# The expert loop of a two-block transformer: 23 items of 128 tokens become 31 items of 64, with each expert's weights loaded once

## The reference, cut to what matters

```python
g_idx = jnp.argmax(t @ w_group + b_group, axis=-1)
top_v, top_i = lax.top_k(e_in_group, 2)
for e in range(16):
    a = silu(t @ w_gate[e]) * (t @ w_up[e])      # 1024 -> 512, twice
    y = y + gates[:, e:e + 1] * (a @ w_down[e])  # 512 -> 1024
```

## Time and profile before

| what | value |
|---|---|
| median of 3 executions | 2894.31 us (2893.11 to 2896.62) |
| span of the profiled execution | 2900.2 us |
| TensorE busy in it | 2738.8 us, 94% |
| VectorE, ScalarE, GpSimd busy | 1274.2, 618.9, 486.6 us |
| moved by DMA | 403.19 MB, 139 GB/s over the span |

### The profile page before, as it was taken

How to read it: one execution, slowest core, us unless ns; L and a number is a source line. 1 busy time by engine, 2 the same in 40 slices (tenths; PEclk the granted TensorE clock), 3 DMA queues, 4 the chain that set the end, 5 groups by cost and what they waited for, 6 DMA issues and landing times.

```text
span 2900.2 us, 36551 instructions
## 1 busy us (share of the span) xinstructions
PE 2738.8 (94%) x14709; PEld 2101.4 (72%) x14709; DVE 1274.2 (44%) x2365; ACT 618.9 (21%) x1184; POOL 486.6 (17%) x515
## 2 busy tenths in 40 slices
PE   7999988897997899999999999999999999999998
PEld 4686755676853688788878877488887585788883
DVE  2072761656354111111132487276663342666651
ACT  2102012242412111111131255211110121211100
POOL 2062600554521000000010006101110001011010
PEclk8999988999998899999999999999999999999999
DMA  9311143243344999899972200122221321322220
GB/s 369 102 44 32 41 146 116 75 152 138 102 175 156 360 333 331 319 328 334 330 266 79 67 7 1 58 73 87 88 80 66 98 88 36 118 87 88 80 80 29
DMA packets 214917, 403.19 MB, mean 139 GB/s; under 512 B 13650, under 2 KB 123778, under 8 KB 205570
## 3 DMA queue, kind: packets, MB, share of 16 engines
q1 hardware_dynamic: 207586, 375.15, 37.7%
q10 hardware_dynamic: 4896, 17.83, 1.5%
q0 software_dynamic: 2304, 8.39, 0.7%
HBM read 369.88 MB, written 31.46 MB: 138 GB/s over the span
## 4 chain that ended last, share of the span: by engine, by line
PE 71%; issue 20%; DVE 3%; ACT 2%; DMA 2%; POOL 1%; SPq 0%; ACTq 0%; POOLq 0%; DVEq 0%
PE ps L2989 18%; PE ps L724 8%; PE ps L1770 6%; PE ps L3063 5%; PE ps L3046 4%; PE ps L2519 4%; PE ps L716 3%; PE ps L3327 3%; PE ps L2676 2%; PE ps L1198 2%; PE ps L415 2%; PE ps L1212 2%; PE ps L796 2%; DMA ring<-in_w_mod 1%; PE ps L2700 1%
## 5 line engine op out<-in xcount | busy, mean ns | idle before, releaser
L2076 PEld LDWEIGHTS ps<-arena,ring 128*128 128x128 f32 x2944 | 334.0, 193 | 14.0 <-issue 10.5
L2076 PE MATMUL ps<-arena,ring 128*128 128x128 f32 x2944 | 334.3, 276 | 3.0 <-DMA ring<-in_w_gate 3.0
L2989 PE MATMUL ps<-arena 128*128 128x256 f32 x1056 | 240.9, 386 | 8.3 <-DVE arena L3145 8.3
L2989 PEld LDWEIGHTS ps<-arena 128*128 128x128 f32 x1056 | 204.5, 194 | 37.5 <-issue 8.7
L724 PE MATMUL ps<-hT,ring 128*128 128x512 f32 x384 | 171.6, 601 | 3.8 <-ACT bet L1075 1.8
L1770 PE MATMUL ps<-ring,hT 128*128 128x512 f32 x384 | 169.7, 598 | 4.6 <-ACT hT L1805 2.4
L2094 PE MATMUL ps<-ring,arena 128*128 128x512 f32 x368 | 164.0, 598 | 1.8
L2989 PE MATMUL ps<-hT,ring 128*128 128x256 f32 x704 | 159.1, 379 | 0.0
L3063 PE MATMUL ps<-ring,arena 128*128 128x512 f32 x352 | 151.7, 592 | 0.0
L2365 DVE TENSOR_TENSOR arena<-arena,ps 128x512 f32<-128x512 f32 x23 | 15.8, 687 | 304.1 <-PE ps L2076 304.1
L2989 PEld LDWEIGHTS ps<-hT,ring 128*128 128x128 f32 x704 | 133.6, 190 | 18.1
(11 more groups left out here) (539 smaller groups left out, 4668.3 us busy)
## 6 DMA issues: line engine op xcount, KB each, us to landing
ring<-in_ada_w SPq DMA_DIRECT2D x48, 1024.0 KB, 5.0
ring<-in_w_gate SPq DMA_DIRECT2D x46, 1024.0 KB, 6.5
ring<-in_w_up SPq DMA_DIRECT2D x46, 1024.0 KB, 5.8
ring<-in_w_down SPq DMA_DIRECT2D x46, 1024.0 KB, 5.4
ring<-in_ffn_w_up SPq DMA_DIRECT2D x44, 1024.0 KB, 5.1
ring<-in_w_mod SPq DMA_DIRECT2D x24, 1024.0 KB, 7.9
ring<-in_w_in SPq DMA_DIRECT2D x18, 1024.0 KB, 8.9
ring<-in_attn_w_in SPq DMA_DIRECT2D x14, 1024.0 KB, 6.0
```

What stands on the lines that cost most here:

```text
L2076: last = pe.matmul(ps[:, t, f * P:(f + 1) * P], w[:, k, f * P:(f + 1) * P], xg[:, 4 * c + k, :], start=(c == 0 and k == 0 and f == 0), sto ...
L2989: last = pe.matmul(ps[:, u % 8, 0:HTOK], a[:, k, :], b[:, k, :], start=(k == 0), stop=(k == KD // 2 - 1))
```

## The change

Items are of 64 tokens: 1024/64 + 15 = 31 of them. An expert with at most one block is given a second, empty one while spare items last; by the counts above every expert then has two items, but expert 13, which has one.

Weights go to `stage`, two halves of 6 MB: the upper part of the arena for even experts, the former ring slots for odd ones. SyncE loads each expert once: gate and up when the last gate/up product of the expert two before is done, down when that one's last down product is done. The first expert's weights are loaded in the stage before (`sp_first_expert`, ahead of the router's weights), the second's once the modulation weights are out of the ring.

On TensorE the 64 tokens are stationary for gate and up: gate in columns 0 to 63 with the gate weights streamed, up in columns 64 to 127 with the up weights streamed, 512 wide, 8 pairs. Down has 4 such pairs, its two halves of output columns side by side. The gate result is tokens by features, so ScalarE copies it out of PSUM and TensorE turns it (`turn_halves`). The first of each pair reads `stage` at an address from a register. The second reads a fixed place: `upw` (two 1 MB halves) and `dnw` (1 MB), which VectorE and ScalarE copy from `stage` for every item. PE, ACT and DVE each read expert table entries into registers in every round. The loop order on TensorE is: gate/up of t+1, turn tokens t+2, down of t, turn halves of t+1.

Outside the loop several semaphores are merged with others, the routing's block arithmetic is done on blocks of 64, the zero rows of `moe_in` take 17 transfers and not 24, and the context weights of the next stage are loaded only after the last gate/up product (`sp_proj`).

```diff
-        arena = sb("arena", [P, ARENA])
+        mem = sb("mem", [P, ARENA + RING * SLOT])
+        arena = mem[:, 0:ARENA]
+        ring = mem[:, ARENA:].rearrange("p (r s) -> p r s", r=RING)
...
-        ITEMS = N_PAIR // P + N_EXP - 1
-        mo = Place(5120)
-        aT = mo(4, P)
-        sg = mo(4, P)
-        xg = mo(KD, P)
-        xt = mo(D)
-        ysb = mo(D)
-        yg = mo(2, NX, D)
+        ITEMS = N_PAIR // HALF + N_EXP - 1
+        BLOCKS = ITEMS + 3
+        STAGE = ARENA - RING * SLOT
+        stage = mem[:, STAGE:].rearrange("p (two x) -> p two x", two=2)
...
+        upw = [at(0, 4, BANK), at(4 * BANK, 4, BANK)]
+        dnw = at(8 * BANK, 4, BANK)
...
+        def piece(par, c):
+            return stage[:, par, c * SLOT:(c + 1) * SLOT].rearrange("p (k n) -> p k n", k=4)
+        def piece_at(par, c, k):
+            return stage[:, bass.ds(par, 1), c * SLOT + k * BANK:c * SLOT + (k + 1) * BANK].rearrange("p a n -> p (a n)")
+        def whole_at(par, c):
+            return stage[:, bass.ds(par, 1), c * SLOT:(c + 1) * SLOT].rearrange("p a n -> p (a n)")
...
+        def sp_expert(sp, e):
+            up = [ins[n][0, e].rearrange("(c k p) n -> c p k n", c=2, p=P) for n in ("w_gate", "w_up")]
+            dn = ins["w_down"][0, e].rearrange("(k p) n -> p k n", p=P)
+            for j, w in enumerate(up):
+                for c in range(2):
+                    sp.dma_start(piece(e % 2, 2 * j + c), w[c]).then_inc(s[f"landing{e % 2}"], 16)
+            if e >= 2:
+                sp.wait_ge(s["down_done"], sp.value_load(etab[0:1, END_AT + e - 2:END_AT + e - 1], min_val=1, max_val=ITEMS))
+            for c in range(2):
+                sp.dma_start(piece(e % 2, 4 + c), dn[:, :, c * BANK:(c + 1) * BANK]).then_inc(s[f"landing{2 + e % 2}"], 16)
+        def sp_first_expert(sp):
+            sp.wait_ge(s["do_out"], 2 * NX)
+            sp_expert(sp, 0)
         def sp_moe(sp, W):
-            sp.wait_ge(s["tokens_sent"], 16 * 2 * NX)
-            sp.dma_start(xt, items_in[0]).then_inc(s["xt_in"], 16)
-            sp.wait_ge(s["item_experts"], 1)
-            with sp.Fori(0, ITEMS) as i:
...
+            sp.wait_ge(s["chunk_used"], W.n)
+            sp_expert(sp, 1)
+            sp.wait_ge(s["routed"], 3)
+            for e in range(2, N_EXP):
+                sp.wait_ge(s["up_done"], sp.value_load(etab[0:1, END_AT + e - 2:END_AT + e - 1], min_val=1, max_val=ITEMS))
+                sp_expert(sp, e)
...
+            def turn_tokens():
 
                 for k in range(KD):
-                    last = pe.transpose(ps[:, 4 + k // 4, (k % 4) * P:(k % 4 + 1) * P], xt[:, k * P:(k + 1) * P], ident[:, :])
-                    if inside:
-                        W.pay(last)
-                return last
+                    last = pe.transpose(ps[:, X_BANK[k // 4], (k % 4) * HALF:(k % 4 + 1) * HALF], xt[:, k * P:(k + 1) * P], ident[0:HALF, 0:HALF])
+                last.then_inc(s["turned"], 1)
+            def gate_up(weights, second):
+                for c in range(2):
+                    if c:
+                        pe.wait_ge(s["item_act"], second)
+                    for k in range(4):
+                        pe.matmul(ps[0:HALF, GU_BANK, :], xg[:, 4 * c + k, :], weights(c, k),
+                                  start=(c == 0 and k == 0), stop=(c == 1 and k == 3), tile_position=(0, 0))
+                        last = pe.matmul(ps[HALF:P, GU_BANK, :], xg[:, 4 * c + k, :], upw[c][:, k, :],
+                                         start=(c == 0 and k == 0), stop=(c == 1 and k == 3), tile_position=(0, HALF))
+                last.then_inc(s["up_done"], 1)
+            def down(weights):
+                for k in range(4):
+                    pe.matmul(ps[0:HALF, Y_BANK, :], aT[:, k, :], weights(k), start=(k == 0), stop=(k == 3), tile_position=(0, 0))
+                    last = pe.matmul(ps[HALF:P, Y_BANK, :], aT[:, k, :], dnw[:, k, :], start=(k == 0), stop=(k == 3),
+                                     tile_position=(0, HALF))
+                last.then_inc(s["down_done"], 1)
+            def turn_halves():
+                for f in range(4):
+                    last = pe.transpose(ps[:, A_BANK, f * P:(f + 1) * P], gu[:, f * P:(f + 1) * P], ident[:, :])
+                last.then_inc(s["turned"], 1)
 
             pe_mods(pe, W, 0, True)
             pe.wait_ge(s["mod_raw"], MGROUPS)
-            assert W.owed
             pe.wait_ge(s["xt_in"], 16)
-            turn_tokens(False).then_inc(s["item_pe"], 1)
-            pe.wait_ge(s["item_dve"], 1)
-            with pe.Fori(0, ITEMS) as i:
...
+            turn_tokens()
+            pe.wait_ge(s["item_dve"], 2)
+            pe.wait_ge(s["item_act"], 2)
+            pe.wait_ge(s["expert_in"], 1)
+            gate_up(lambda c, k: piece(0, c)[:, k, :], 1)
+            pe.wait_ge(s["xt_in"], 32)
+            turn_tokens()
+            pe.wait_ge(s["item_act"], gu_copied(0))
+            turn_halves()
+            pe.wait_ge(s["item_dve"], 4)
+            pe.wait_ge(s["routed"], 3)
+            with pe.Fori(0, ITEMS - 1) as t:
+                landed = pe.value_load(etab[0:1, bass.ds(t + (E_AT + 1), 1)], min_val=1, max_val=2 * N_EXP - 1)
+                par = pe.value_load(etab[0:1, bass.ds(t + (PAR_AT + 1), 1)], min_val=0, max_val=1)
+                pe.wait_ge(s["expert_in"], landed)
+                pe.wait_ge(s["item_dve"], tokens_dve(t + 1))
+                pe.wait_ge(s["item_act"], tokens_act(t + 1))
+                gate_up(lambda c, k: piece_at(par, c, k), second_copied(t + 1))
+                pe.wait_ge(s["xt_in"], t * 16 + 48)
+                landed_before = pe.value_load(etab[0:1, bass.ds(t + E_AT, 1)], min_val=1, max_val=2 * N_EXP - 1)
+                par_before = pe.value_load(etab[0:1, bass.ds(t + PAR_AT, 1)], min_val=0, max_val=1)
+                turn_tokens()
+                pe.wait_ge(s["expert_in"], landed_before + 1)
+                pe.wait_ge(s["item_dve"], product_ready(t))
+                down(lambda k: piece_at(par_before, 4, k))
+                pe.wait_ge(s["item_act"], gu_copied(t + 1))
+                turn_halves()
...
+            down(lambda k: piece_at(last_par, 4, k))
...
+            def up_copy(src):
+                a.activation(upw[1].rearrange("p k n -> p (k n)"), src, ACT.Copy).then_inc(s["item_act"], 1)
+            def gu_copy():
+                a.activation(gu, ps[:, GU_BANK, :], ACT.Copy).then_inc(s["item_act"], 1)
...
+            with a.Fori(0, ITEMS - 1) as t:
+                landed = a.value_load(etab[0:1, bass.ds(t + (E_AT + 2), 1)], min_val=1, max_val=2 * N_EXP - 1)
+                par = a.value_load(etab[0:1, bass.ds(t + (PAR_AT + 2), 1)], min_val=0, max_val=1)
+                a.wait_ge(s["up_done"], t + 2)
+                gu_copy()
+                a.wait_ge(s["expert_in"], landed)
+                up_copy(whole_at(par, 3))
+                a.wait_ge(s["turned"], tokens_turned(t + 2))
+                modulated()
+                tokens(items_in[bass.ds(t + 3, 1), :, :].rearrange("a p d -> p (a d)"))
+                a.wait_ge(s["turned"], halves_turned(t + 1))
+                gate_silu()
+                a.wait_ge(s["item_dve"], weighed_ready(t))
+                out_halves(items_out[bass.ds(t, 1), :, :].rearrange("a p d -> p (a d)"))
...
+            NT = SEQ // HALF
...
+            ch.link(v.tensor_scalar(spare_n[:, 0:1], c_e[:, 0, N_EXP - 1:N_EXP], -1.0, float(ITEMS), ALU.mult, ALU.add))
+            ch.link(v.scalar_tensor_tensor(out=ends[:, 1:], in0=c_e[:, 1, :], scalar=spare_n[:, 0:1], in1=c_e[:, 0, :],
+                                           op0=ALU.min, op1=ALU.add))
...
+            with v.Fori(0, ITEMS - 1) as t:
+                landed = v.value_load(etab[0:1, bass.ds(t + (E_AT + 2), 1)], min_val=1, max_val=2 * N_EXP - 1)
+                par = v.value_load(etab[0:1, bass.ds(t + (PAR_AT + 2), 1)], min_val=0, max_val=1)
+                landed_down = v.value_load(etab[0:1, bass.ds(t + (E_AT + 1), 1)], min_val=1, max_val=2 * N_EXP - 1)
+                par_down = v.value_load(etab[0:1, bass.ds(t + (PAR_AT + 1), 1)], min_val=0, max_val=1)
+                v.wait_ge(s["up_done"], t + 2)
+                v.wait_ge(s["expert_in"], landed)
+                up_copy(whole_at(par, 2))
+                v.wait_ge(s["turned"], tokens_turned(t + 2))
+                modulated()
+                v.wait_ge(s["down_done"], t + 1)
+                v.wait_ge(s["item_out"], t * 32 + 32)
+                weighed()
+                v.wait_ge(s["expert_in"], landed_down + 1)
+                down_copy(whole_at(par_down, 5))
+                v.wait_ge(s["turned"], halves_turned(t + 1))
+                v.wait_ge(s["item_act"], silu_ready(t + 1))
+                gated()
...
+            for e in range(N_EXP):
+                g.wait_ge(s[f"landing{e % 2}"], 64 * (e // 2 + 1))
+                g.sem_inc(s["expert_in"], 1)
...
+            sp.wait_ge(s["up_done"], ITEMS)
```

(27 more changed lines are left out.)

311 lines of the change are left out of this document (168 added, 143 removed).

## The result

The changed kernel takes 2763.93 us (median of 4 runs, 2762.17 to 2771.99) against 2894.54 of the kernel before: a ratio of 0.9547, with a 95% interval of 0.9528 to 0.9565, 130.6 us less. The forecast was 2774, 120 us less.

The account below looks back on a forecast made before the run. TensorE sets the loop's pace, DMA close behind. Loop from 978.3 + 30 x 12.4 + 1 = 1351.3, with the tail in effect 1366 against 1485.95: 120 us less, 2774 us from 2894.3; range 2750 to 2850.

Parts of the forecast that it names:

- A pair's pass of 0.43 us: TensorE, gate/up and down: two column groups' passes run together in 0.43 us, giving 6.9 and 3.4 us an item.
- rival of no overlap: TensorE pairs: the second matmul waits for the first, 10.3 us more an item, 3093 us in all; chance 0.11.
- a register's address might keep the next pass back until the pipe is empty: Rival, TensorE pairs: passes follow only after the pipe empties, 121 us more, 2895 us, no change; chance 0.06.
- A share of 2.38 for three column groups: Counter-rule for TensorE pairs: a pass of an estimated 0.54 us, an item 2.7 us more, the forecast 83 us later.
- The item: Expert loop on TensorE: 12.4 us an item, between 12.0 and 12.6, as gate/up, down, turning and changes.
- the transposes and the changes: TensorE, each item: 12 transposes at 0.11 us, 1.3 us; four column-group/whole-array changes at 0.2, 0.8 us.
- What fits beside it: Between gate/up products: ACT's chain of about 4.1 us in 5.3, 1.2 to spare; DVE's copy 1.3 to 2.3 us.
- The table load that the rival feared: ACT: a 1.28 us table load between copy and modulation uses up the slack; copies-or-registers rival 2792 to 2846 us, chance 0.20.
- DMA: Loop traffic: 117 MB, 355 us at 330 GB/s, under TensorE's 384; rival that DMA sets the pace 2810 us, chance 0.05.
- The stall behind the expert of one item: Loop, expert 13: its 12.4 us item against 12.7 us plus landing for the next gate and up weights, 1 us stall.
- Ahead of the loop: Last scatters and token load: expert 1's load delays them 5.4 us (bounds 0 and 8), first turning at 962.0.
- The end: After the loop: last silu, product and down 4.7 us, then 7 to the gather, 3 more from context loads.

Follow-up runs that it names:

- e10: Changed kernel with both matmuls of each pair in column group 0, into two banks, copy out and product in two pieces: 3078.4 us.
- e6: Changed kernel with ACT's 2048-column copy made twice in the loop, the first to a place nobody reads: 2784.88 us.
- e2: Changed kernel with each weight chunk of experts 1 to 15 moved a second time, to a DRAM place nobody reads: 2922.2 us.
- e4: Changed kernel without spare items for experts with at most one block; eight experts have one item, seven empty items stand at the end: 2800.64 us.
- e8: e3, plus gate and up waiting for ACT only ahead of their second half, and DVE modulating before it copies: 2756.26 us.
- e3: Changed kernel with SP issuing expert 1's load only once the first tokens have been read: 2761.2 us.
- after: The changed kernel itself, first profiled execution: 2765.31 us.
- after_again: The changed kernel once more, nothing altered: 2766.01 us, ratio 0.9545 to the kernel before.
- before_again: The kernel before the change once more, nothing altered: 2892.54 us.
- e12: The e8 version of the changed kernel once more, run beside e11: 2756.91 us.
- e9: Changed kernel with all eight gate matmuls ahead of all eight of up, and down four and four: 2973.95 us.
- e1: Changed kernel, same column groups, but the four matmuls of one half in a row ahead of the other's four: 2872.71 us.
- e11: The e8 version, with context loads from the fourth on waiting for the first gather to land instead of the last down product: 2754.28 us.

## Why the prediction was right, point by point

- **A pair's pass of 0.43 us.** Right, and with it nearly all of the gain: 16 rounds of gate and up in 7.02 us with the change behind them (forecast 6.9 + 0.2), 8 of down in 3.58 (3.4 + 0.2). The rival of no overlap is e10, forecast at 3093 and measured at 3078, so its price was right and its chance the only question. That a register's address might keep the next pass back until the pipe is empty isn't so either: passes with such an address start every 0.43 us. A share of 2.38 for three column groups, which the prediction cites from the Trainium skill (TensorE: Matmul & The Clock Gate, Part 3, Measured speedup vs the span model), would have made the pass an estimated 0.54 us: not so here (0.43 for two groups), nor for four groups in the earlier trace rows.
- **The item: 12.4 us forecast, 11.83 measured**, under its own lower bound of 12.0. The mis-sized terms are the transposes and the changes. Eight transposes of 64 tokens take 0.71 us from the first start to the last end where those of 128 took 1.04, so they start about every 0.07 us, not every 0.11: turning and the change behind it take 0.64 together, for 0.88 + 0.2. "That the 64-token ones stream half the columns I count as nothing" was the step: it is worth some 0.3 us an item. Gate and up with their change take 7.02 = 16 x 0.43 + 0.14, down 3.58 = 8 x 0.43 + 0.14, the four full-width transposes with theirs 0.59 = 4 x 0.11 + 0.15, while behind the eight of tokens some 0.08 is left. So a change is about 0.14, once 0.08, and not 0.2, which is the other 0.3 us. Over 30 items 0.57 us makes 17 us. (The range's upper sum of 2787 should read 2785; nothing rests on it.)
- **What fits beside it.** ACT's slack was put at 1.2 us and is 1.1, by the timeline and by e6. DVE's copy takes 1.23 us (forecast 1.3 to 2.3). The register loads show in no wait of TensorE. The table load that the rival feared comes once in the loop, at 971.72, and no more.
- **DMA.** 92.4 MB on SP's queue and 16.1 on ACT's between 955 and 1335, forecast 117, which counts the loads of experts 0 and 1 that began before 955. Not the bound, as said. The step "Both are near their limit" was too strong, though: e2 moves 391 GB/s, and the earlier trace rows already had 399 in one stretch.
- **The stall behind the expert of one item: 1 us forecast, 4.0 measured.** The forecast set 12.7 us of transfer and its landing against one item of 12.4. In the trace the room is wider, 16.5 us (from the issue at 1264.52, right behind the product that frees the place, to 1281.1, when gate and up would have started), but the transfer takes 15.7, and behind its landing stand in series ACT's copy of 1.92 and its modulation of 1.28, with their handovers some 3.4. These were left out, as were the 1.4 us at the lower clock behind the wait. e4 adds six more of these waits, e8 removes most of this one.
- **Ahead of the loop.** The first turning at 955.42 with the 6.8 us of the execution added is 962.2, forecast 962.0. e3 shows that the reason was right too: with expert 1's load kept back the turning comes 3.5 us sooner, and all the delay behind the last scatter is gone. That the size fits to 0.2 us is luck in part: the prediction's 2.7 MB would take 8.2 us at 330 GB/s, and nothing it shows leads to 5.4; the traces have 4.5 us (after) and 3.4 (after_again) behind the last scatter. From the first turning to the second gate and up it took 16.4 us (forecast 16.3), and here two errors cancel: turning and modulation took 2.5 (3.4), the first product and the uncovered chain 13.9 (12.9).
- **The end.** From the last gate and up to the last down it took 13.87 us, the down itself 5.3, together 19.2 (forecast 17.1: an item of 12.4, then 4.7 for the last silu, product and down). The down waited 2.0 us for DVE's product and then ran at the lower clock; two of its passes are

```profile
1335.30 1.06 PE L2146 MATMUL ps<-mem,hT 128*64 128x512 f32 x1
...
1336.15 1.06 PE L2146 MATMUL ps<-mem,hT 128*64 128x512 f32 x1
```

They are 0.85 us apart and not 0.43. From there to the first gather's issue 7.8 us (7). The landing of 8.41 in the chain of waits isn't the first gather's and not to be set against the 5.77 of the earlier trace rows: it is the fourth's, issued at 1351.32, the other the second's, issued at 1487.25. From the first issue DVE starts after 8.85 us (1347.50 to 1356.35), before after 7.35 (1485.95 to 1493.30), and the next stage's products start after 41.4 us, before after 39.2 and in before_again after 39.7. So the context loads cost some 2 us here, forecast 3.

**The sum.** From the second gate and up (971.86) to the end of the last down (1339.7) it took 367.8 us, forecast 377.7: 9.9 less, which is -17.1 for the item, +3.0 for the stall, +1.7 for the second item (13.52 us, at 0.80 of the clock behind its wait of 3.38 us) and +2.6 for the last item's uncovered chain and its slow down product: -9.8. The other terms agree within 1 us, or cancel as said. So the forecast was 10 us late of a gain of 130, by the item alone, and the errors of stall and clock hid a part of what the item was wrong by.

What stays open: why the last down runs at full clock in e8, e12 and e9 and partly at the lower one in the change (both traces), e1, e3, e4, e6 and e11, behind the same wait of 2.0 us; and whether two streams that both come from a register's address would overlap too. That last was not tried: here the second stream always lies in a copy at a fixed address.

## What to carry to other kernels

With two column groups of 64, two fp32 matmuls with different streams of 512 columns run in the time of one, so a half-filled stationary costs half, not all: items can be cut to the size of the data. This holds only if the two groups' matmuls alternate in the code; rows of eight passes of one group in front of the other gave 109 of the 131 us back, rows of sixteen more than all. Before you count on it, ask what is left beside the shorter item: which copies run between two of its products, and whether its weights still fit under it where an item stands alone, with everything that is in series behind the landing.

## What the runs showed of the hardware

- A matmul of one column group starts while up to about four passes of the other stand ahead of it in program order (e1: items of 15.47 us; e9: 18.79; alternating: 11.83; one group: 22.11), measured for groups of 64 and 512 streamed columns. Its passes thus start out of the code's order: in e9 up's first at 1114.85, gate's last, which the code puts ahead of it, at 1116.13.
- A change between half-width and full-width matmuls costs about 0.14 us in three of an item's four places and 0.08 behind the transposes of 64 tokens (periods of 7.02, 3.58, 0.59 and 0.64 us in the trace of the change).
- Transposes of 64 tokens start every 0.07 us, those of 128 every 0.11.
- The 16 DMA engines moved 391 GB/s over 380 us (e2, partly from DRAM to DRAM), where 330 looked like a limit.
- Waits of 12.0, 3.4, 2.5 and 2.0 us of TensorE were each followed by passes at the lower clock, waits of 0.5 us (e8) and of 0.9 and 0.7 (e12) by none; the one of 2.0 us only in some traces. With one column group at a time, so half of the columns in use, the granted clock was 1.00 over 400 us (e10), as with both.
